# Statistics per row block, staged output stores and a prefetch of the next x tile in a decoder layer on eight cores

## The reference

```
x = x + 1/2 * SwiGLU_1(rmsnorm(x))                # FFN1, D_FF = 2816
h = rmsnorm(x); z = h @ w_in                       # mixer: window attention, recurrent block, memory attention
merged = sum_b sigmoid(gate_b(h)) * (y_b @ W_b_o); x = x + merged @ w_out
x = x + 1/2 * SwiGLU_2(rmsnorm(x))                # FFN2
y = rmsnorm(x) * final_norm
rmsnorm(x, g) = x * rsqrt(mean(x*x) + 1e-6) * g
```

## Time and profile before

| | |
|---|---|
| median of 2 runs | 5498.73 us (5411.11 and 5586.35) |
| profiled execution | 5409.97 us |
| span of its slowest core | 5408.9 us |
| TensorE busy | 3916.2 us, 72% |
| VectorE busy | 1717.0 us, 32% |
| ScalarE busy | 1105.0 us, 20% |
| GpSimd busy | 694.2 us, 13% |
| mean granted TensorE clock | 0.820 to 0.828 of full speed on the eight cores |

### The profile page before, as it was taken

The page is one execution under the profiler, slowest core; times in us unless marked ns, Lnnn a source line. Parts: engine busy times, 40 slices in busy tenths (PEclk is TensorE's granted clock), DMA queues, the critical chain, the costliest instruction groups (busy, mean ns, idle before and its releaser), DMA issues.

```text
span 5408.9 us, 54261 instructions; the slowest of 8 cores (5326.5 to 5408.9 us)
## 1 busy us (share of the span) xinstructions
PE 3916.2 (72%) x20020; PEld 1883.8 (35%) x20020; DVE 1717.0 (32%) x2337; ACT 1105.0 (20%) x1920; POOL 694.2 (13%) x782
## 2 busy tenths in 40 slices
PE   0657788878787878787888798879887988723322
PEld 0223334433343434343434343434433443312321
DVE  0113511451135222622262226322542245203420
ACT  0103211331133112311131113211321132100010
POOL 0100111111110111011101110111011101120001
PEclk9877899789887988798969896989798988955556
DMA  9946599649964997398819892989378946895459
GB/s 162 132 69 86 81 141 129 92 68 123 158 94 63 129 139 113 57 133 133 127 29 136 129 132 38 122 129 139 49 106 133 137 85 88 121 153 133 141 83 152
DMA packets 769977, 603.38 MB, mean 112 GB/s; under 512 B 19996, under 2 KB 755865, under 8 KB 767297
## 3 DMA queue, kind: packets, MB, share of 16 engines
q0 software_dynamic: 726064, 498.84, 68.8%
q1 hardware_dynamic: 43657, 101.06, 6.8%
HBM read 1072.45 MB, written 45.67 MB: 207 GB/s over the span
## 4 chain that ended last, share of the span: by engine, by line
PE 60%; DMA 18%; DVE 11%; issue 3%; ACT 3%; another core or an unknown queue 3%; POOL 1%; SPq 1%; DVEq 0%; ACTq 0%; POOLq 0%
PE ps L320 60%; DMA sb_wsl<-ffn_w_gu 7%; DVE sb_scr L332 3%; DMA sb_wsl<-w_in 2%; DVE sb_scr L1026 2%; ACT sb_junk L323 1%; DMA sb_wsl<-ffn_w_down 1%; DMA sb_xres<-x 1%; DMA sb_k<-ck 1%; DMA y<-sb_xres 1%; DVE sb_xres L332 1%; DVE sb_scr L637 1%; DVE sb_k L335 1%; ACT sb_pb L323 1%
## 5 line engine op out<-in xcount | busy, mean ns | idle before, releaser
L320 PE MATMUL ps<-sb_hT,sb_wsl 128*128 128x512 bf16 (+2 forms) x10016 | 2072.2, 369 | 308.8 <-DMA sb_wsl<-ffn_w_gu 213.4
L320 PEld LDWEIGHTS ps<-sb_hT,sb_wsl 128*128 128x128 bf16 x10016 | 925.5, 100 | 1446.0 <-issue 454.0
L320 PE MATMUL ps<-sb_wsl,sb_actT 128*128 128x512 bf16 (+1 forms) x2904 | 642.6, 384 | 31.6 <-DMA sb_wsl<-ffn_w_down 31.6
L335 DVE TENSOR_TENSOR sb_actT<-sb_scr,ps 128x512 bf16<-128x512 f32 (+1 forms) x396 | 250.4, 632 | 1249.8 <-PE ps L320 1220.5
L320 PE MATMUL ps<-sb_identb,sb_actT 128*128 128x128 bf16 (+1 forms) x808 | 101.7, 302 | 539.7 <-DVE sb_actT L327 537.9
L323 ACT ACTIVATE sb_scr<-ps 128x512 f32<-128x512 f32 (+1 forms) x396 | 218.8, 553 | 1226.3 <-PE ps L320 1226.0
L126 POOL DMA_DIRECT2D sb_wsl<-ffn_w_gu x396 | 360.3, 919 | 798.3 <-PE ps L320 798.2
L320 PEld LDWEIGHTS ps<-sb_wsl,sb_actT 128*128 128x128 bf16 (+1 forms) x2904 | 285.3, 98 | 385.6 <-issue 50.4
L323 ACT ACTIVATE sb_junk<-sb_xres 128x1024 bf16<-128x1024 f32 (+1 forms) x134 | 141.6, 1056 | 1098.4 <-DVE sb_xres L332 755.6
L332 DVE SCALAR_TENSOR_TENSOR sb_xres<-ps,sb_xres 128x512 f32<-128x512 f32 (+1 forms) x198 | 136.9, 691 | 657.1 <-PE ps L320 657.1
L126 POOL DMA_DIRECT2D sb_wsl<-w_in x153 | 141.3, 925 | 1567.9 <-PE ps L320 1567.9
(11 more groups left out here) (131 smaller groups left out, 2740.9 us busy)
## 6 DMA issues: line engine op xcount, KB each, us to landing
sb_wsl<-ffn_w_gu POOLq DMA_DIRECT2D x396, 512.0 KB, 15.5
sb_wsl<-ffn_w_down POOLq DMA_DIRECT2D x72, 1024.0 KB, 11.1
sb_wsl<-w_in POOLq DMA_DIRECT2D x71, 1024.0 KB, 10.6
sb_wsl<-w_in POOLq DMA_DIRECT2D x74, 768.0 KB, 12.2
sb_wsl<-ffn_w_down POOLq DMA_DIRECT2D x36, 768.0 KB, 9.9
sb_wsl<-w_out POOLq DMA_DIRECT2D x18, 1024.0 KB, 12.5
sb_xres<-x SPq DMA_DIRECT2D x8, 2048.0 KB
y<-sb_xres SPq DMA_DIRECT2D x8, 2048.0 KB
```

The source lines that it names most:

```text
L320: P.add("pe", lambda e: e.matmul(out, lhsT, rhs, start=start, stop=stop, skip_group_check=True), reads, writes)
L335: P.add("dve", lambda e: e.tensor_tensor(out=out, in0=in0, in1=in1, op=op), reads, writes)
```

## The change

norm_stats is new and is called by norm_to_hT and final_norm_store: for each row block a Square, a mean and a power, each with its own name (("ss", tb), ("ms", tb), ("rstd", tb)). The buffer junk is now a view of chunks 20 and 21 of actT and carries their names. Two staging buffers ystage of 128 x 1024 f32 are new. final_norm_store multiplies a row block into ystage[tb % 2], stores it by a 512 KB DMA, and then, if there is a next tile, issues the 512 KB load of the same row block of the next tile's x into xres. A prompt tile loads x itself only if that was not done before it (tile 0), in four DMAs. Half 1 of the down-projection and of the output projection accumulates in PSUM banks 0 to 3; half 0 stays in 4 to 7.

```diff
--- before.py
+++ after.py
@@ -259,8 +259,10 @@
 
     wsl = [sb(f"wsl{i}", [128, 8, 512], BF16) for i in range(NW)]
     xres = [sb("xres0", [128, 4, D], F32)]
-    junk = sb("junk", [128, D], BF16)
     AT = sb("actT", [128, 22 * 512], BF16)
+    junk = AT[:, 20 * 512:22 * 512]
+    JK = [("actT", 20), ("actT", 21)]
+    ystage = [sb(f"ystage{i}", [128, D], F32) for i in range(2)]
     hT = sb("hT", [128, 8, 512], BF16)
     QM = sb("QM", [128, 8, 512], BF16)
     k01 = sb("k01", [128, 4, 2, 512], BF16)
@@ -464,17 +466,21 @@
         pass
 
 
+    def norm_stats(cx):
+        nr, ntb = cx.nr, cx.ntb
+        for tb in range(ntb):
+            act(junk[0:nr, :], xres[0][0:nr, tb, :], AF.Square, xk(tb), JK + [("ss", tb)], accum_out=stat[0:nr, tb:tb + 1])
+            dve_ts(stat[0:nr, 8 + tb:9 + tb], stat[0:nr, tb:tb + 1], 1.0 / D, 1e-6, ALU.mult, ALU.add, [("ss", tb)], [("ms", tb)])
+            P.add("pool", lambda e, o=stat[0:nr, 16 + tb:17 + tb], i0=stat[0:nr, 8 + tb:9 + tb], i1=chalf[0:nr, 0:1]: e.tensor_tensor(out=o, in0=i0, in1=i1, op=ALU.pow),
+                  [("ms", tb), "chalf"], [("rstd", tb)])
+
     def norm_to_hT(cx, gcol):
         nr, ntb, N = cx.nr, cx.ntb, cx.N
-        for tb in range(ntb):
-            act(junk[0:nr, :], xres[0][0:nr, tb, :], AF.Square, xk(tb), ["junk", ("ss", tb)], accum_out=stat[0:nr, tb:tb + 1])
-        dve_ts(stat[0:nr, 8:8 + ntb], stat[0:nr, 0:ntb], 1.0 / D, 1e-6, ALU.mult, ALU.add, [("ss", t) for t in range(ntb)], ["ms"])
-        P.add("pool", lambda e: e.tensor_tensor(out=stat[0:nr, 16:16 + ntb], in0=stat[0:nr, 8:8 + ntb], in1=chalf[0:nr, 0:ntb], op=ALU.pow),
-              ["ms", "chalf"], ["rstd"])
+        norm_stats(cx)
         CK("m2a")
         for tb in range(ntb):
             dve_ts(AT[0:nr, tb * D:(tb + 1) * D], xres[0][0:nr, tb, :], stat[0:nr, 16 + tb:17 + tb], None, ALU.mult, None,
-                   xk(tb) + ["rstd"], [("actT", 2 * tb), ("actT", 2 * tb + 1)])
+                   xk(tb) + [("rstd", tb)], [("actT", 2 * tb), ("actT", 2 * tb + 1)])
         CK("m2b")
         for kc in range(8):
             b = genbank()
@@ -502,12 +508,14 @@
                 kcs = list(range(8 * g3, min(8 * g3 + 8, 22)))
                 s = wload([(wd[128 * kcs[0]:128 * (kcs[-1] + 1), 512 * half:512 * half + 512], 0, len(kcs), 512, 128)])
                 for tb in range(ntb):
+                    pb_ = (4 if half == 0 else 0) + tb
                     for i, kc in enumerate(kcs):
-                        mm(ps[4 + tb][0:nr, :], actc(kc)[:, tb * 128:tb * 128 + nr], wsl[s][:, i, 0:512], kc == 0, kc == 21,
-                           wk(s) + [("actT", kc)], [("ps", 4 + tb)])
+                        mm(ps[pb_][0:nr, :], actc(kc)[:, tb * 128:tb * 128 + nr], wsl[s][:, i, 0:512], kc == 0, kc == 21,
+                           wk(s) + [("actT", kc)], [("ps", pb_)])
             for tb in range(ntb):
+                pb_ = (4 if half == 0 else 0) + tb
                 xs_ = xres[0][0:nr, tb, half * 512:(half + 1) * 512]
-                dve_stt(xs_, ps[4 + tb][0:nr, :], 0.5, xs_, ALU.mult, ALU.add, [("ps", 4 + tb), ("x", tb, half)], [("x", tb, half)])
+                dve_stt(xs_, ps[pb_][0:nr, :], 0.5, xs_, ALU.mult, ALU.add, [("ps", pb_), ("x", tb, half)], [("x", tb, half)])
 
     def proj_fm(cx, col0, ncols, consume):
         N = cx.N
@@ -701,27 +709,27 @@
         for half in range(2):
             s = wload([(wout_d[:, 512 * half:512 * half + 512], 0, 8, 512, 128)])
             for tb in range(ntb):
+                pb_ = (4 if half == 0 else 0) + tb
                 for kc in range(8):
-                    mm(ps[4 + tb][0:nr, :], QM[:, kc, tb * 128:tb * 128 + nr], wsl[s][:, kc, 0:512], kc == 0, kc == 7, wk(s) + [("QM", kc)], [("ps", 4 + tb)])
+                    mm(ps[pb_][0:nr, :], QM[:, kc, tb * 128:tb * 128 + nr], wsl[s][:, kc, 0:512], kc == 0, kc == 7, wk(s) + [("QM", kc)], [("ps", pb_)])
             for tb in range(ntb):
+                pb_ = (4 if half == 0 else 0) + tb
                 xs_ = xres[0][0:nr, tb, half * 512:(half + 1) * 512]
-                dve_stt(xs_, ps[4 + tb][0:nr, :], 0.5, xs_, ALU.mult, ALU.add, [("ps", 4 + tb), ("x", tb, half)], [("x", tb, half)])
-
-    def final_norm_store(cx, ydst):
+                dve_stt(xs_, ps[pb_][0:nr, :], 0.5, xs_, ALU.mult, ALU.add, [("ps", pb_), ("x", tb, half)], [("x", tb, half)])
+
+    def final_norm_store(cx, ydst, after_tb=None):
         nr, ntb = cx.nr, cx.ntb
+        norm_stats(cx)
         for tb in range(ntb):
-            act(junk[0:nr, :], xres[0][0:nr, tb, :], AF.Square, xk(tb), ["junk", ("ss", tb)], accum_out=stat[0:nr, tb:tb + 1])
-        dve_ts(stat[0:nr, 8:8 + ntb], stat[0:nr, 0:ntb], 1.0 / D, 1e-6, ALU.mult, ALU.add, [("ss", t) for t in range(ntb)], ["ms"])
-        P.add("pool", lambda e: e.tensor_tensor(out=stat[0:nr, 16:16 + ntb], in0=stat[0:nr, 8:8 + ntb], in1=chalf[0:nr, 0:ntb], op=ALU.pow),
-              ["ms", "chalf"], ["rstd"])
-        for tb in range(ntb):
-            dve_stt(xres[0][0:nr, tb, :], xres[0][0:nr, tb, :], stat[0:nr, 16 + tb:17 + tb], gfin[0:nr, :], ALU.mult, ALU.mult,
-                    xk(tb) + ["rstd", "gfin"], xk(tb))
-        if cx.mode == "prompt":
-            P.dma("sp", ydst.rearrange("(tb p) d -> p tb d", p=128), xres[0][:, :, :], reads=[k for t in range(4) for k in xk(t)])
-        else:
-            P.dma("sp", ydst, xres[0][0:nr, 0, :], reads=xk(0))
-
+            ys_ = ystage[tb % 2]
+            dve_stt(ys_[0:nr, :], xres[0][0:nr, tb, :], stat[0:nr, 16 + tb:17 + tb], gfin[0:nr, :], ALU.mult, ALU.mult,
+                    xk(tb) + [("rstd", tb), "gfin"], [("yst", tb % 2)])
+            if cx.mode == "prompt":
+                P.dma("sp", ydst[tb * 128:(tb + 1) * 128, :], ys_[:, :], reads=[("yst", tb % 2)])
+            else:
+                P.dma("sp", ydst, ys_[0:nr, :], reads=[("yst", tb % 2)])
+            if after_tb is not None:
+                after_tb(tb)
 
     def cache_shift_copies():
         for g in range(3):
@@ -1038,11 +1046,17 @@
         while hooks:
             hooks.pop(0)()
 
+    PRELOAD = [False]
+
     def prompt_tile(j):
         cx = Ctx(); cx.nr, cx.ntb, cx.N, cx.mode, cx.nseq, cx.L = 128, 4, TN, "prompt", 1, TN
         N = TN
         s_, b_, slot = j % 4, j // 4, j % 2
-        P.dma("sp", xres[0][:, :, :], x_d[j * TN:(j + 1) * TN, :].rearrange("(tb p) d -> p tb d", p=128), writes=[k for t in range(4) for k in xk(t)])
+        def load_x(jj, tb):
+            P.dma("sp", xres[0][:, tb, :], x_d[jj * TN + tb * 128:jj * TN + (tb + 1) * 128, :], writes=xk(tb))
+        if j == 0 or not PRELOAD[0]:
+            for tb in range(4):
+                load_x(j, tb)
         CK(f"t{j}_load")
         norm_to_hT(cx, R_G1)
         CK(f"t{j}_norm1")
@@ -1133,7 +1147,9 @@
         CK(f"t{j}_merge")
         norm_to_hT(cx, R_G2)
         ffn(cx, w2gu_d, w2d_d)
-        final_norm_store(cx, y_d[j * TN:(j + 1) * TN, :])
+        nxt = (lambda tb: load_x(j + 1, tb)) if (j + 1 < ntiles) else None
+        PRELOAD[0] = nxt is not None
+        final_norm_store(cx, y_d[j * TN:(j + 1) * TN, :], after_tb=nxt)
 
     try:
         setup()
```

## The result

The change made the kernel 0.6% faster: the ratio of the times after and before is **0.9942, with a 95% interval of 0.9929 to 0.9954**. On the 5410 us of the profiled execution before that is 31 us (25 to 38). The median of all runs went from 5498.84 to 5378.71, but that difference is mostly not the kernel's: executions of both kernels fall into an undisturbed group (5406 to 5411 before, 5374 to 5382 after) and a disturbed one 3% and more above it, the two medians caught different shares of them, and the ratios in this document compare undisturbed ones alone. The profiled execution after took 5377.11 (span 5375.9, core 0), 33 us less than before.

The account below looks back on a forecast made before the run. Bound by TensorE, whose stops at normalisations end with weights issued after GpSimd's last power. Boundaries −59, mixer +17, FFN2 −4, first tile −3 sum to −49 us: 5409.97 to 5361; range 5325 to 5400, reaching 5450 with run spread.

Parts of the forecast that it names:

- the aliased junk: After an FFN, no Square starts before TensorE's last matmul: 2.9 us lost per normalisation, +17 us in all before the mixer.
- weights behind the last power set every restart: At normalisations, TensorE waits for weights issued only after GpSimd's last power; the first boundary's stop is 44.7 us.
- Rival C: At normalisations, per-block work is off the path and only aliasing counts, if hT ends the waits: 5343 us; chance 0.10.
- multiplies stand behind the fourth mean: In VectorE's order the first scaling multiply still follows the fourth mean, so only the power leaves that path.
- the banks: Half 1 of down- and output projection in banks 0 to 3: cost 0, or one add of 0.69 us.
- 4 MB still want about 17.0 − 2 × 2.5 (...) = 12 us, plus one 2.5, after 1.45: landed at 16: Tile boundary: last x load lands 16 us after the last mean; gain 11.3 per boundary, 8.4 less aliasing, −59 in all.
- its lower bound: Boundary: 512 KB pieces don't disturb each other; multiplies 2 and 3 wait for stores, last load lands at 12.5 us.
- the rate argument: Boundary: DMA share of 0.82 and 0.72 means engines mostly taken by one direction, so 4 MB want about 12 us.
- the last one is over 0.46 us earlier relative to the last mean: GpSimd's last small power ends 0.46 us earlier at each normalisation; before FFN2 worth 8 × 0.46 = −4 us.
- come every 1.24 us, so GpSimd keeps up: At each normalisation the four small powers arrive at the Squares' pace, 1.24 us, each taking 0.56, so none queue.
- the base: Whole kernel: forecast counted from the profiled execution, 5409.97 us, 1.6% below the median shown, 5498.73.

Follow-up runs that it names:

- Experiment 9: Changed kernel with the four weight loads after each normalisation of a prompt tile put ahead of its statistics in GpSimd's list; ratio 0.9707 to the kernel before.
- experiment 11: Changed kernel with Square output in hT, four staging buffers and weight loads ahead of statistics, but only two of four ahead of the final norm; 0.9582.
- experiments 1 and 4: 1: changed kernel with Square output in hT instead of actT, 0.9873. 4: the same with one mean and one power per normalisation, 0.9881.
- experiment 8: Kernel before with the bank edit alone (half 1 of down- and output projection in PSUM banks 0 to 3); ratio 0.9988.
- Experiment 6: Changed kernel with four staging buffers, as f32 views of actT, instead of two; ratio 0.9923 to the kernel before.
- Experiment 7: Changed kernel without the stores of y of tiles 0 to 6; ratio 0.9852 to the kernel before.
- Experiment 5: Changed kernel in which every scaling and output multiply waits for all four powers; ratio 0.9924 to the kernel before.
- experiment 10: Changed kernel with Square output in hT, four staging buffers and the four weight loads ahead of the statistics together; ratio 0.965 to the kernel before.

## Why the prediction was right or wrong

**Right: the aliased junk.** 2.9 us after every FFN; seen in the profile (means 5.13 instead of 2.2 us after the last matmul), and shown by adding it (+49 us) and by taking it away (−37).

**Right: weights behind the last power set every restart.** Experiment 9 moved only that order and won 127 us. Rival C (hT and not the weights) falls: on the slowest cores before and after, the weights ended every one of these waits, and on all eight cores all but 4 of 176 before and 1 of 176 after, these few before the mixer. In experiment 11, with the first weights there in time, TensorE starts 0.06 us after its last transpose group.

**Right: multiplies stand behind the fourth mean,** so splitting the statistics brings little (experiments 1 and 4), and the banks bring nothing (experiment 8).

**Wrong: the step "4 MB still want about 17.0 − 2 × 2.5 (...) = 12 us, plus one 2.5, after 1.45: landed at 16".** The landing measured 17.2. I had taken a start and an end part of 2.5 us off both store and load and put one back, as if such parts of one direction would lie under the other. From the first store's issue to the landing it is 17.2 − 1.4 = 15.8 us, against 17.0 for store and load one after the other and the 14.5 of the sum. So overlap was put at 2.5 us and is worth 1.2. Experiment 6 shows where most of the missing 1.3 went: with four buffers it is 16.3 − 1.3 = 15.0. The waits of multiplies 2 and 3 for the stores, which the step left out though its lower bound had them, cost 0.8 to 0.9, and the rate argument itself was off by 0.4 to 0.5. The gain of 9.7 at this step (26.9 to 17.2) comes mostly from elsewhere: 1.3 + 4.9 − 1.3 = 4.9 from the power and three multiplies that no longer precede the transfers, 3.7 from the Squares that run while x lands, 1.1 from overlap. Experiment 7 shows the sharing: without the stores x lands at 10.8. Error: 1.2 x 7 = 9 us.

**Wrong: the step "the last one is over 0.46 us earlier relative to the last mean".** Its duration was right, 0.55 us, with VectorE idle. But the edit also lets VectorE's multiplies start beside it, and then it takes 1.26 or 1.51. It ends 1.3 to 1.5 us after the last mean, where the old one of 1.03 ended at 1.2. Experiment 5 shows this cause before the mixer (0.37 us back with VectorE idle), but not before FFN2 (0.03 back). Before FFN2 the statement that the powers "come every 1.24 us, so GpSimd keeps up" failed too, as three means come at once; how much of the miss there that makes is open. Errors: 0.4 x 7 before the mixer, 0.35 x 8 before FFN2, 0.3 x 7 at the boundary, 7 to 8 us together.

The two errors are 9 + 8 = 17 of the 18 us between forecast (−49) and measurement (−31). They are read from issue and landing times of one core in each kernel, and the −31 is the middle of 25 to 38, so that the sum closes to one microsecond is luck.

**Wrong: the base.** The forecast time, 5361, was counted from the lower of two runs that differed by 3.2%, while the median lay between them. Read against that median it promised 2.5%, though the argument held only 0.9%, and 0.6% was measured. The prediction had said so itself and kept the lower run.

## What to carry to other kernels

When a scratch output is moved into a live buffer, look up who reads that buffer last: it inherits all their waits, and here the 2 KB cost 37 of the 69 us that the rest of the change won. Before splitting a small operation to pipeline it, look at the order in which its engine executes the pieces, and at what starts beside it once it is off the path. If every restart of the bounding engine is released by a transfer, ask first what stands ahead of its issue in the queue, and then how many bytes share the gap: half of the weights ahead beat all of them. A shorter stop can win more than its length, if the engine comes back at a higher clock.

## What the runs showed of the hardware

A small operation on GpSimd that starts behind a multiply of VectorE is held up by it. A 128x1 power takes 0.55 us alone, 1.26 beside 128x1024 f32 to bf16 scalings, 1.51 beside 128x1024 f32 products of two SBUF operands. The multiplies are not slower beside a power: two products take 2.48 us there, and four took 4.87 without one before, both one every 1.2 us. Beside GpSimd's DMA issues it is the scalings that are slower: they come every 0.97 us (four in 3.67 before), and the first three after the change, mostly ahead of the issues, every 0.66. The transposes show it, first of the changed kernel:

```profile
810.79 0.27 PE L322 MATMUL ps<-sb_identb,sb_actT 128*128 128x128 bf16 x1 [25.58 <-DVE sb_actT L329]
...
811.45 0.27 PE L322 MATMUL ps<-sb_identb,sb_actT 128*128 128x128 bf16 x1 [0.40 <-DVE sb_actT L329]
812.11 0.26 PE L322 MATMUL ps<-sb_identb,sb_actT 128*128 128x128 bf16 x1 [0.40 <-DVE sb_actT L329]
813.08 3.11 PE L322 MATMUL ps<-sb_identb,sb_actT 128*128 128x128 bf16 x29 [0.71 <-DVE sb_actT L329]
```

then at the same place in experiment 10, where no weights are issued:

```profile
788.29 0.27 PE L323 MATMUL ps<-sb_identb,sb_actT 128*128 128x128 bf16 x1 [30.33 <-DVE sb_actT L330]
788.95 0.26 PE L323 MATMUL ps<-sb_identb,sb_actT 128*128 128x128 bf16 x1 [0.40 <-DVE sb_actT L330]
789.61 0.27 PE L323 MATMUL ps<-sb_identb,sb_actT 128*128 128x128 bf16 x1 [0.40 <-DVE sb_actT L330]
790.27 3.25 PE L323 MATMUL ps<-sb_identb,sb_actT 128*128 128x128 bf16 x29 [0.40 <-DVE sb_actT L330]
```

Each transpose starts when a scaling is done: at 0.66 and 0.66, then 0.97 beside the issues; without them all come 0.66 apart. The Trainium skill (SBUF — State Buffer, SBUF: two separate sides) says that the two engines share a pair of ports, and that of a GpSimd operation and a VectorE operation in a two-port mode or with two SBUF inputs whichever starts first holds it for its whole instruction. For the products the trace agrees: at the first boundary the power starts with 1.0 us of the product's 1.2 still to go and takes 0.96 longer than alone, and at 1889.71 us of the same core, where the power starts 0.24 us ahead of the product, it takes 0.55. For the scalings it agrees less well. The excess is 0.71 us, a whole scaling of 0.66, though 0.2 of it is over when the power starts; and before FFN2 the third power starts 0.24 us ahead of the first scaling and still takes 1.03. That rule spoke against the 0.46 us of the prediction, which did not use it.

Loads and stores between HBM and SBUF that are in flight together took 15.8 us for 2 MB each way, 15.0 with four staging buffers, against 17.0 in sequence and 9.5 (10.8 − 1.3) for the load without the store. All eight cores did this at the same time. The two directions together saved 1.2 to 2.0 us over one after the other.
